# Queries of the expert layer by lists of 128 columns, with 31 single-row slots between them

## The chip, the cores and the metric

The kernel runs on one core of a Trainium2 chip. The metric is the device time of one execution in microseconds; lower is better. Times come from the kernel's timed executions and from one profiled execution.

## What is computed

Two transformer-like blocks run one after the other on 256 tokens of width 2048. The change lies at the end of the second block, in its last projection and its layer of 16,384 experts:

```
x_lat = x_lat + m_lat[2] * (y_l @ w_out[l])
hf = modulate(rmsnorm_2(x_lat, norm_ffn[l]), m_lat[3], m_lat[4])   # h * (1 + scale) + shift
x_lat = x_lat + m_lat[5] * peer_ffn(hf, ...)
# peer_ffn:
q = (ht @ wq).reshape(n, 8, 2, 128)          # 8 heads, 2 halves: 16 lists of 128 columns
s = einsum('nhpc,pkc->nhpk', q, keys)        # 128 scores for each token and list
# top 16 of each half, top 16 of their 256 sums: 16 experts a head, 128 slots a token
gate = softmax(sc)
a = einsum('nd,nhkd->nhk', xb, take(u_tab, eb))
out = einsum('nhk,nhkd->nd', gate * gelu(a), take(v_tab, eb))
```

Each token picks 128 experts (slots). A slot needs its row of U (2048 floats, for a dot product with the token) and its row of V (2048 floats, added to the output with the slot's weight). Then comes a last RMS norm.

## The kernel before

Tokens are handled as two blocks of 128, one token per partition. Dense products stream their weights from memory in chunks of 1 MB (128 partitions x 2048 floats, four chunks to a tile of 512 columns) through four slots. For each chunk ScalarE writes a rounded high part (`hi`, L1273), VectorE the low part (`lo`, L1879), and TensorE does `products` (L691, L692, L695): for each of 4 slices of 128 input rows and each of 2 token blocks three products (high x high, high x low, low x high) with the activations stationary and 512 weight columns moving. SyncE reloads a slot once TensorE has counted the chunk in `split_used`.

At the end of the second block four output tiles (`add_gated` adds them to X and squares them) are followed by the norm, `scaled` (X times the reciprocal root), `queries_turned` (transposes on TensorE), `queries_part` (scale, shift, split in high and low), and 16 chunks of the query product in four tiles. After each tile the 512 query columns are copied to `q_tok`, turned, copied to `q_t`, and multiplied with the keys (L1234); ScalarE copies the scores to `key_s`. `modulated` (L2728, L2730) makes the token rows for the dots. `choose` (top 16 by MAX8, FIND_INDEX8 and MATCH_REPLACE8, then the pick by one-hot products) writes the expert numbers of one or two heads to `idx`. `weights` and `exps` make the softmax. `low_part` (L654) has GpSimd make the low part of four of the 16 chunks.

`GATHERS` is the order in which GpSimd issues the row gathers (indirect DMA, L665). The first 12 slots of token block 0 are gathered as a U row each (1 MB for 128 tokens), into three homes in turn; their V rows come later as single rows. All slots after that are pairs: U and V row together, 2 MB, in seven homes. Four of these homes are the weight slots, two the activations' high and low parts, so they come free only as the last query chunks are done. The last six slots of block 1 are single again. A gather waits until its home has been used (`half_used`): a U row by its dot (`dot`, L2737, on VectorE), a V row or a pair by its sum. The sum of a slot is four TensorE products of 512 columns with a diagonal matrix of the slot's weight (L1259); ScalarE makes that matrix (`diagonal`: gelu L1841, weight L1826, matrix L1829). Before, all sums come after the whole query product. A slot goes: gather, dot, diagonal, sum, next gather into its home.

Of the kernel before, what the change touches and what calls it, by code (L numbers as in the profile page):

```python
# [15 lines left out]
P = 128  # L16
# [58 lines left out]
EARLY_DOTS = (0, 0, 0, 0, 0, 0, 1, 2, 1, 2, 1, 2, 1, 2, 0, 0)  # L75
EARLY_V_AT = 20
DIAGS = 4
POOL_LO = (9, 11, 13, 15)
POOL_LO_AT = (3, 6, 9, 12)
NFIN_AT = 24  # L80
# [66 lines left out]
NCH = S_WQ + OUT_TILES * CPT  # L147
# [66 lines left out]
def homes():  # L214

    places, halves = [], 0
    for kind, b, s in GATHERS:
        if kind == "u" and b == 0:
            places.append(EARLY_HOMES[s % len(EARLY_HOMES)])
# [26 lines left out]
def build(nc, a, out):  # L246
    with ExitStack() as ctx:
# [26 lines left out]
        for name, n in (("ident", P), ("cols", 512), ("modt", 12 * KT), ("small", 512), ("X", NB * D), ("UH", KT * T),  # L274
                        ("UL", KT * T), ("RW", 2 * SLOTS_W * D), ("P", 12288),
                        ("TMP", 6176), ("C", 3584), ("MISC", 1120)):
            region[name] = words
            words += n
# [7 lines left out]
        cols = view("cols", "cols", 0, [512])  # L286
        modt = view("modt", "modt", 0, [6 * KT, 2])
        X = view("X", "X", 0, [NB, D])
        UH = view("UH", "UH", 0, [KT, T], F32R)
        UL = view("UL", "UL", 0, [KT, T], F32R)  # L290
# [120 lines left out]
        assert -(-NCOL // 8) * 8 + P <= 512  # L411
# [5 lines left out]
        q_tok = view("q_tok", "P", 8192, [NB, CW])  # L417
        q_t = view("q_t", "P", 8192 + NB * CW, [2 * GH, T])
        rest = view("rest", "P", 10240, [CK, T])
        key_s = [view("key_s0", "C", 0, [2 * PH, NKEY]), view("key_s1", "TMP", 0, [2 * PH, NKEY])]  # L420
        cand = view("cand", "C", 2048, [GH, TOPK, TOPK])
        hot = view("hot", "C", 2048 + GH * TOPK * TOPK, [GH, TOPK, TOPK])
# [5 lines left out]
        pick_i = view("pick_i", "MISC", 256, [GSTEP], U32)  # L428
        pick_f = view("pick_f", "MISC", 288, [GSTEP])
        exp_f = [view(f"exp_f{i}", "MISC", 320 + 32 * i, [GSTEP]) for i in range(2)]  # L430
# [9 lines left out]
        nfin_rows = view("nfin_rows", "MISC", 400, [CW])  # L440
        sq_out = view("sq_out", "C", 0, [D])
        low_ps, y_ps = [psum[:, 4 * j:4 * j + 4, :].rearrange("p a c -> p (a c)") for j in range(2)]
        rows_g = view("rows_g", "UH", 0, [max(PAIR_AT) + 1, D])
        assert region["UH"] + 14 * D == region["P"] + 4096
# [21 lines left out]
        def half_used(g, half):  # L466

            earlier = [k for k in range(g) if HOMES[k][0] == HOMES[g][0] and (GATHERS[k][0] == "p" or HOMES[k][1] == half)]
            if earlier:
                return dotted(earlier[-1]) if GATHERS[earlier[-1]][0] == "u" else summed(earlier[-1])  # L470
            if HOMES[g] in EARLY_HOMES:
                return sem("xn2_ready"), NB
            return split_used, NCH - SLOTS_W + PAIR_CHUNK[HOMES[g][0]]
# [77 lines left out]
        def hdim(x):  # L551
            return x[:, :].unsqueeze(2)

# [36 lines left out]
        def _(pool):  # L590
# [60 lines left out]
            def low_part(c):  # L651
                s = (S_WQ + c) % SLOTS_W
                pool.wait_ge(hi_ready, S_WQ + c + 1)
                pool.tensor_tensor(WL[:, s, :], raw[:, s, :], WH[:, s, :].bitcast(F32), ALU.subtract).then_inc(sem("pool_lo"), 1)  # L654

            for g, (kind, b, s) in enumerate(GATHERS):
                if g in POOL_LO_AT:
                    low_part(POOL_LO[POOL_LO_AT.index(g)])
# [17 lines left out]
        def _(pe):  # L676
            def products(n, banks, k0, nk, i, per, ah, al, blocks=NB, first=True, last=True, each=None):

                if i is None and n - S_WQ in POOL_LO:
                    pe.wait_ge(sem("pool_lo"), POOL_LO.index(n - S_WQ) + 1)  # L680
                elif i is not None or n:
                    pe.wait_ge(lo_ready, lin(n + 1 - sum(S_WQ + c < n for c in POOL_LO), i, per))
# [514 lines left out]
            linear_among(S_OUT2, Q_OUT2, 0, OUT_TILES, last_turned(), ready=lambda m: (sem("y2_ready"), CK * (m + 1)))  # L1197

            SIDE = ACC[(Q_WQ + 1) % 2]

            def queries_turned(r):
                pe.wait_ge(sem("xn_ready"), NB * xn_made[5] + r + 1)
                if r == 0:
                    for k in range(CK):
                        for b in range(NB):
                            mm = pe.transpose(DB[k][:, b * P:(b + 1) * P], XN2[:, b, k * P:(k + 1) * P], ident[:, :])
                        if k % 2:
                            mm.then_inc(sem("xn_turned"), 1)
                    return
                if r >= 2:  # L1210
                    pe.wait_ge(sem("u_ready"), KT * 4 + CK * (r - 1))
                turn_part(r, XN2, SIDE if r == 1 else DB[2 * (r % 2):2 * (r % 2) + 2])

            def stay_warm(n):
                for _ in range(n):
                    pe.matmul(DB[3][:, 0:NB * P], ident_b[:, :], mask_b[:, :, :].rearrange("p d t -> p (d t)"), start=True, stop=True)

            def queries():
                until = clock(0)
                for r in range(2, CPT):  # L1220
                    queries_turned(r)
                    yield from until(r - 1)
                for t in range(OUT_TILES):
                    yield from until(CPT * (t + 1))
                    pe.wait_ge(acc_free_act, Q_WQ + t + 3)
                    pe.wait_ge(acc_free_dve, Q_WQ + t + 3)
                    turn(lambda j, m: q_tok[:, m % 2, (2 * j + m // 2) * P:(2 * j + m // 2 + 1) * P], DB[0:2], "pq_turned")
                    yield from until(CPT * (t + 1) + 1)
                    pe.wait_ge(sem("q_t_ready"), 2 * (t + 1))
                    if t:  # L1230
                        pe.wait_ge(sem("key_s_ready"), 2 * t)
                    for b in range(NB):
                        for hp in range(2 * GH):
                            mm = pe.matmul(DB[2 + b][:, hp * NKEY:(hp + 1) * NKEY], q_t[:, hp, span(b)],  # L1234
                                           keys[:, hp % 2, :], start=True, stop=True)
                        mm.then_inc(sem("key_ps"), 1)

            stay_warm(40)
            queries_turned(0)
            queries_turned(1)  # L1240
            linear_among(S_WQ, Q_WQ, 0, OUT_TILES, queries(), ready=u_parts(4, 1),
                         each=lambda k: (sem("u_ready"), KT * 4 + k + 1))

            for n, g in enumerate(SUMS):
                kind, b, s = GATHERS[g]
                if n == NFIN_AT:
                    pe.wait_ge(sem("nfin_landed"), 16)
                    pe.wait_ge(sem("key_s_ready"), 2 * OUT_TILES)
# [12 lines left out]
                mm.then_inc(sem("v_done"), 1)  # L1261


        @block.scalar
        def _(act):
# [487 lines left out]
            def outputs():  # L1753
# [5 lines left out]
                for t in range(OUT_TILES):  # L1759
                    if t == OUT_TILES - 1:  # L1760
                        act.activation(spare[:, :], l_ms[0][:, 0:1], ACT.Sqrt)
                    yield from until(CPT * (t + 1) + 2)
                    w = slice(t * CW, (t + 1) * CW)
                    act.wait_ge(acc_free_dve, Q_OUT2 + t + 3)
                    act.activation(XN2[:, 1, w], X[:, 1, w], ACT.Square, accum_out=ss_part[:, 1, t:t + 1]).then_inc(
                        sem("ss_ready"), 1)

            linear_among(S_OUT2, Q_OUT2, 0, OUT_TILES, nothing, outputs())
# [3 lines left out]
            SIDE = ACC[(Q_WQ + 1) % 2]  # L1772

            def queries_part(r):
                if r == 0:
                    act.wait_ge(split_used, S_WQ)
                    for k in range(CK):
                        act.wait_ge(sem("xn_turned"), 8 * 4 + k // 2 + 1)
                        act.activation(UH[:, k, :], DB[k][:, 0:T], ACT.Identity, scale=sc_ffn[:, k:k + 1],
                                       bias=modt[:, 3 * KT + k, 0:1]).then_inc(sem("uh_ready"), 1)  # L1780
                    return
                turned_part(r, 4, SIDE if r == 1 else DB[2 * (r % 2):2 * (r % 2) + 2], lambda k: sc_ffn[:, k:k + 1],
                            lambda k: modt[:, 3 * KT + k, 0:1], S_WQ)

            queries_part(0)
            queries_part(1)
# [1163 lines left out]
```

## Time and profile before

| | before |
|---|---|
| median of the timed runs | 2998.67 us (2998.47 to 3000.13) |
| profiled execution, its own time | 3002.66 us |
| span of its records | 3001.0 us |
| TensorE busy | 2664.9 us, 89% |
| VectorE busy | 2058.4 us, 69% |
| moved by the DMA engines | 958.74 MB |

Times in the rows are microseconds from the span's start. "x16" is a count of records; a float32 product that isn't rounded leaves two records of TensorE, each with its weight load. "[2.03 <-X]" is idle time before a row and what ended it.

### The profile page before, as it was taken

To read this page: it belongs to the slowest core of one execution; us is meant where nothing else is said; L and a number is where in the kernel's file an instruction comes from. 1 tells how busy PE (TensorE), PEld (TensorE's weight loads), DVE (VectorE), ACT (ScalarE), POOL (GpSimd) and SP (SyncE) were. 2 spreads that over 40 slices of the span, in tenths; PEclk is the share of its full clock that TensorE was granted. 3 is DMA by queue.
4 is the path that set the end of the run, shared out by engine and by line. 5 is a ranking of instruction groups with operands and counts; after the bars stand their busy time and mean duration, and the time that the engine had idled before them with its cause. 6 is when DMAs were issued, how large, how long until landed. Compare 5 with 4: busy or idle time off the path is not lost.

```text
span 3001.0 us, 28457 instructions
## 1 busy us (share of the span) xinstructions
PE 2664.9 (89%) x10052; PEld 1807.8 (60%) x10052; DVE 2058.4 (69%) x2510; ACT 1055.7 (35%) x1584; POOL 386.1 (13%) x401
## 2 busy tenths in 40 slices
PE   9999999999999999999999889877777777777773
PEld 7888888888888878888788754322222222222221
DVE  6675689999999987666566894676664554444446
ACT  5544443433333455635454422222222121111111
POOL 0000000000000000000000353211211121111112
PEclk9999999999999999999999999999999999999997
DMA  6454779888888964444354699999999999999997
GB/s 250 170 207 169 282 266 333 330 324 340 333 337 336 343 259 169 150 151 168 130 198 176 229 389 426 428 428 427 429 428 428 428 428 427 428 428 428 427 428 324
DMA packets 99086, 958.74 MB, mean 319 GB/s; under 512 B 11044, under 2 KB 11364, under 8 KB 13608
## 3 DMA queue, kind: packets, MB, share of 16 engines
q0 software_dynamic: 55552, 650.96, 52.2%
q1 hardware_dynamic: 43280, 305.91, 27.6%
q8 instruction: 61, 1.00, 0.1%
q10 hardware_dynamic: 152, 0.53, 0.0%
q14 instruction: 41, 0.34, 0.0%
HBM read 955.23 MB, written 2.13 MB: 319 GB/s over the span
## 4 chain that ended last, share of the span: by engine, by line
PE 59%; DMA 30%; DVE 7%; issue 2%; ACT 2%; POOL 0%; POOLq 0%; SPq 0%; DVEq 0%; ACTq 0%
DMA rows_g<-in_uv_tab_dram,idx 30%; PE bank L691 16%; PE bank L695 16%; PE bank L692 16%; PE bank L1259 6%; DVE rows_g L2737 4%; PE bank L725 1%; PE bank L1074 0%; PE bank L1019 0%; PE bank L733 0%; ACT diag L1829 0%; DMA ctx_x<-in_ctx_dram 0%; DVE split L1879 0%; POOL rows_g L665 0%; DMA raw<-in_wstream_dram 0%
## 5 line engine op out<-in xcount | busy, mean ns | idle before, releaser
L1259 PE MATMUL bank<-rows_g,diag 128*128 128x512 f32 x2000 | 918.7, 605 | 270.9 <-ACT diag L1829 270.9
L2737 DVE CUSTOM_DVE_ANT_0 rows_g<-rows_g,XN 128x2048 f32<-128x2048 f32 x256 | 596.7, 2333 | 542.1 <-DMA rows_g<-in_uv_tab_dram,idx 540.3
L1259 PEld LDWEIGHTS bank<-rows_g,diag 128*128 128x128 f32 x2000 | 365.0, 191 | 824.2 <-issue 824.0
L1879 DVE TENSOR_TENSOR split<-raw,split 128x2048 fp32r<-128x2048 f32 x282 | 645.3, 2289 | 283.6 <-ACT split L1273 277.7
L1273 ACT ACTIVATE split<-raw 128x2048 fp32r<-128x2048 f32 x286 | 547.8, 1917 | 674.3 <-DMA raw<-in_wstream_dram 661.9
L691 PE MATMUL bank<-split,UH 128*128 128x512 f32 x1936 | 764.5, 395 | 3.1 <-DVE split L1879 2.7
L695 PE MATMUL bank<-split,UL 128*128 128x512 f32 x1936 | 755.2, 390 | 0.0
L692 PE MATMUL bank<-split,UH 128*128 128x512 f32 x1936 | 754.6, 390 | 0.0
L665 POOL DMA_INDIRECT rows_g<-in_uv_tab_dram,idx x274 | 301.4, 1100 | 1080.9 <-PE bank L1259 858.5
L691 PEld LDWEIGHTS bank<-split,UH 128*128 128x128 f32 x1936 | 364.4, 188 | 79.1 <-issue 3.2
L695 PEld LDWEIGHTS bank<-split,UL 128*128 128x128 f32 x1936 | 364.1, 188 | 76.5
L692 PEld LDWEIGHTS bank<-split,UH 128*128 128x128 f32 x1936 | 364.3, 188 | 73.9
L1841 ACT ACTIVATE gelu_v<-dots 128x1 f32<-128x1 f32 x238 | 48.2, 203 | 927.7 <-DVE dots L2737 927.6
L2156 DVE CUSTOM_DVE_ANT_0 ada_out<-ada_w,c_row 128x2048 f32<-128x2048 f32 x128 | 292.2, 2283 | 0.0
L606 POOL DMA_DIRECT2D ada_w<-in_ada_dram x96 | 50.7, 528 | 695.0 <-DVE ada_sum L2156 695.0
L691 PE MATMUL bank<-split,FH 128*128 128x512 f32 x320 | 124.6, 389 | 0.2 <-DVE X L2224 0.2
L695 PE MATMUL bank<-split,FL 128*128 128x512 f32 x320 | 124.5, 389 | 0.0
L692 PE MATMUL bank<-split,FH 128*128 128x512 f32 x320 | 124.5, 389 | 0.0
L1829 ACT ACTIVATE diag<-ident,slot_w 128x128 f32<-128x128 f32 x250 | 100.3, 401 | 8.2
L1826 ACT ACTIVATE slot_w<-gelu_v,gate_w 128x1 f32<-128x1 f32 x250 | 73.4, 294 | 7.8
L691 PEld LDWEIGHTS bank<-split,FH 128*128 128x128 f32 x320 | 60.1, 188 | 13.0 <-DVE X L2224 0.4
L695 PEld LDWEIGHTS bank<-split,FL 128*128 128x128 f32 x320 | 60.1, 188 | 12.5
(417 smaller groups left out, 1442.2 us busy)
## 6 DMA issues: line engine op xcount, KB each, us to landing
raw<-in_wstream_dram SPq DMA_DIRECT2D x287, 1024.0 KB, 4.9
ada_w<-in_ada_dram POOLq DMA_DIRECT2D x96, 1024.0 KB, 7.1
rows_g<-in_uv_tab_dram,idx POOLq DMA_INDIRECT x274, 26.2
X<-in_x_dram SPq DMA_DIRECT2D x4, 512.0 KB, 9.4
c_row<-in_c_rows_dram POOLq DMA_DIRECT2D x1, 2048.0 KB, 8.5
ctx_x<-in_ctx_dram POOLq DMA_DIRECT2D x1, 2048.0 KB, 11.6
gb<-mod_rows POOLq DMA_DIRECT2D x2, 1024.0 KB, 5.9
raw<-in_wstream_dram SPq DMA_DIRECT2D x2, 512.0 KB, 6.7
```

Source lines behind the costliest of these rows:

```text
L606: pool.dma_start(ada_w[s][:, :], a["ada"][c]).then_inc(ada_landed[s], 16)
L665: pool.indirect_dma_start(out=whole(g) if kind == "p" else row(g), out_offset=None, in_=a["uv_tab"], in_offset=bass.IndirectOffsetOnAxis(a ...
L691: pe.matmul(o, ah[:, k0 + k, t], wh[:, w], start=first and k == 0, stop=False)
L692: mm = pe.matmul(o, ah[:, k0 + k, t], wl[:, w], start=False, stop=al is None and last and k == nk - 1)
L695: mm = pe.matmul(o, al[:, k0 + k, t], wh[:, w], start=False, stop=last and k == nk - 1)
L1259: mm = pe.matmul(bank[4 * b + c], diag[:, n % DIAGS, :], v[:, c * CW:(c + 1) * CW], start=n in (0, SUMS_0), stop=n + 1 in (SUMS_0, len(SUMS)))
L1273: act.activation(WH[:, n % SLOTS_W, :], raw[:, n % SLOTS_W, :], ACT.Copy).then_inc(hi_ready, 1)
L1826: seq(act.activation(slot_w[:, b, s:s + 1], gelu_v[:, b, s:s + 1], ACT.Copy, scale=gate_w[:, b, s:s + 1]))
L1829: act.activation(diag[:, n % DIAGS, :], ident[:, :], ACT.Copy, scale=slot_w[:, b, s:s + 1]).then_inc(sem("diag_ready"), 1)
L1879: dve.tensor_tensor(WL[:, n % SLOTS_W, :], raw[:, n % SLOTS_W, :], WH[:, n % SLOTS_W, :].bitcast(F32), ALU.subtract).then_inc(lo_ready, 1)
L2156: dve.tensor_tensor_reduce(ada_out[:, :], ada_w[ada_slot(c)][:, :], c_row[:, r, :], 1.0, 0.0, ALU.mult, ALU.add, ada_sum[:, p:p + 1]).then ...
L2737: dve.tensor_tensor_reduce(row(g), row(g), x, 1.0, 0.0, ALU.mult, ALU.add, dots[:, b, s:s + 1]).then_inc(sem("dot_done"), 1)
```

## The change

The weights of the query product become the stationary operand and the turned activations the moving one: 16 lists of 128 query columns, one chunk of 1 MB each, 16 slices x 3 products with 258 columns moving (two blocks of 128 tokens and two columns that hold the shift). The result is already turned, so `q_tok`, its transposes and the four tiles go. X times `sc_row` is turned without the norm, while the last output tile runs; the norm comes back as a row `rms_row` in `query` and as a scale in `scores_kept`. The dummy products (`stay_warm`) and GpSimd's `low_part` go. `choose` does its two one-hot picks together. 31 first slots are single U and V rows, with two homes for U and two for V. The first is summed ahead of list 6, and 30 after the thirds of lists 6 to 15. The first pair, slot 31, is issued behind the V row of slot 30, which waits for the sum of slot 28.

```diff
-PAIR_AT = (4, 6, 14, 8, 10, 0, 2, 17)
+PAIR_AT = (4, 6, 14, 8, 10, 0, 2, 16)
-EARLY, LATE = 12, 6
-EARLY_HOMES = ((2, 0), (2, 1), (PAIRS, 0))
+LATE = 6
+LISTS = 2 * PH
+MIX_AT, MIX = 6, 3
+EARLY = 1 + MIX * (LISTS - MIX_AT)
+U_HOMES, V_HOMES = ((2, 0), (PAIRS, 0)), ((PAIRS, 1), (2, 1))
-NFIN_AT = 24
+NFIN_AT = 64
 def gathers():
-    order = [("u", 0, s) for s in range(EARLY)]
-    for s in range(EARLY, SLOTS):
-        order.append(("p", 0, s))
-        k = s - EARLY_V_AT
-        if k % 2 == 0 and 0 <= k < EARLY:
-            order += [("v", 0, k), ("v", 0, k + 1)]
+    order = [("u", 0, 0)]
+    for s in range(EARLY):
+        if s + 1 < EARLY:
+            order.append(("u", 0, s + 1))
+        order.append(("v", 0, s))
+    order += [("p", 0, s) for s in range(EARLY, SLOTS)]
...
+            def list_part(c, k0, k1):
+                s = (S_WQ + c) % SLOTS_W
+                o = q_bank(c)[:, 0:T + SHIFT]
+                for k in range(k0, k1):
+                    w = slice(k * P, (k + 1) * P)
+                    pe.matmul(o, WH[:, s, w], UHS[:, k, :], start=k == 0, stop=False)
+                    pe.matmul(o, WL[:, s, w], UHS[:, k, :], start=False, stop=False)
+                    mm = pe.matmul(o, WH[:, s, w], ULS[:, k, :], start=False, stop=k == KT - 1)
+                if k1 == KT:
+                    mm.then_inc(split_used, 1)
+            def list_scores(c):
+                pe.wait_ge(sem("q_t_ready"), c + 1)
...
+            last_output_tile()
+            first_list()
+            for c in range(1, MIX_AT):
+                list_begins(c)
+                at = KT // 4 if c == 2 else KT // 2
+                list_part(c, 0, at)
+                if c < 3:
+                    list_scores(c - 1)
+                elif c > 3:
+                    list_scores(c - 2)
+                list_part(c, at, KT)
+            sum_row(0)
+            for c in range(MIX_AT, LISTS):
+                list_begins(c)
+                for j in range(MIX):
+                    list_part(c, KT * j // MIX, KT * (j + 1) // MIX)
+                    if j == 0:
+                        list_scores(c - 2)
+                    sum_row(1 + MIX * (c - MIX_AT) + j)
...
+            lo(S_WQ + 2)
+            query(0)
+            lo(S_WQ + 3)
+            modulated(0)
+            query(1)
+            lo(S_WQ + 4)
+            for _ in choose(0, 0, 0, 1):
+                pass
+            query(2)
+            lo(S_WQ + 5)
+            query(3)
+            modulated(1)
+            weights(0, 0, TOPK)
+            lo(S_WQ + 6)
+            query(4)
+            dve.wait_ge(sem("xn2_ready"), NB)
+            dot(DOTS[0], XN2[:, 0, :])
+            dot(DOTS[1], XN2[:, 0, :])
+            lo(S_WQ + 7)
+            query(5)
+            early = early_choices()
+            for c in range(MIX_AT, LISTS):
+                for j in range(MIX):
+                    n = 2 + MIX * (c - MIX_AT) + j
+                    if n < EARLY:
+                        dot(DOTS[n], XN2[:, 0, :])
+                    next(early, None)
+                    if j == 1:
+                        lo(S_WQ + c + LEAD)
+                query(c)
```

## Rows read from the trace of the kernel before

**Rows 1.** The page: busy shares, then DMA rate in 40 slices.

```profile
PE 2664.9 (89%) x10052; PEld 1807.8 (60%) x10052; DVE 2058.4 (69%) x2510; ACT 1055.7 (35%) x1584; POOL 386.1 (13%) x401
GB/s 250 170 207 169 282 266 333 330 324 340 333 337 336 343 259 169 150 151 168 130 198 176 229 389 426 428 428 427 429 428 428 428 428 427 428 428 428 427 428 324
```

**Rows 2.** Windows: length, busy time of each engine, PE clock, DMA share, GB/s.

```profile
1690.00:1747.30 57.30, 43.90 (x205) 36.23 (x204) 43.66 (x34) 16.03 (x15) 44.58 (x17) 0.91 0.86 325
1747.30:1760.00 12.70, 11.56 (x54) 9.33 (x53) 12.32 (x35) 2.09 (x4) 7.54 (x4) 1.00 0.77 308
1760.00:2975.00 1215.00, 928.05 (x2032) 371.42 (x2032) 681.41 (x974) 250.57 (x773) 268.85 (x258) 0.99 1.01 428
```

**Rows 3.** Timeline of VectorE: two dots of the pair stage.

```profile
2048.96 2.29 DVE L2737 CUSTOM_DVE_ANT_0 rows_g<-rows_g,XN 128x2048 f32<-128x2048 f32 x1 [2.59 <-DMA rows_g<-in_uv_tab_dram,idx]
2053.85 2.29 DVE L2737 CUSTOM_DVE_ANT_0 rows_g<-rows_g,XN 128x2048 f32<-128x2048 f32 x1 [2.59 <-DMA rows_g<-in_uv_tab_dram,idx]
```

**Rows 4.** Timeline of GpSimd: the first gather, a split, the first pair.

```profile
1693.83 2.08 POOL L665 DMA_INDIRECT rows_g<-in_uv_tab_dram,idx  x1 [130.93 <-DVE idx L2722]
...
1727.68 4.61 POOL L654 TENSOR_TENSOR split<-raw,split 128x2048 fp32r<-128x2048 f32 x1
...
1747.27 2.82 POOL L665 DMA_INDIRECT rows_g<-in_uv_tab_dram,idx  x1 [0.16 <-issue]
```

**Rows 5.** Timeline of TensorE and VectorE around the norm and the first choice.

```profile
1637.60 4.54 PE L1216 MATMUL bank<-mask_b,ident_b 128*128 128x256 bf16 x40
1682.88 0.49 DVE L2680 MAX8 top_v<-key_s 128x8 f32<-128x128 f32 x2 [0.16 <-DVE XN L2730]
1692.66 0.17 DVE L2722 CAST idx<-pick_f 128x16 uint32<-128x16 f32 x1
```

**Rows 6.** Groups by line: count, busy, mean ns, idle before.

```profile
L2737 DVE CUSTOM_DVE_ANT_0 rows_g<-rows_g,XN 128x2048 f32<-128x2048 f32 x256 | 596.7, 2333 | 542.1 <-DMA rows_g<-in_uv_tab_dram,idx 540.3
L1879 DVE TENSOR_TENSOR split<-raw,split 128x2048 fp32r<-128x2048 f32 x282 | 645.3, 2289 | 283.6 <-ACT split L1273 277.7
L1273 ACT ACTIVATE split<-raw 128x2048 fp32r<-128x2048 f32 x286 | 547.8, 1917 | 674.3 <-DMA raw<-in_wstream_dram 661.9
raw<-in_wstream_dram SPq DMA_DIRECT2D x287, 1024.0 KB, 4.9
```

**Rows 7.** Timeline of TensorE and its weight loads: spacing of products.

```profile
1565.97 0.39 PE L695 MATMUL bank<-split,UL 128*128 128x512 f32 x1
1566.19 0.39 PE L691 MATMUL bank<-split,UH 128*128 128x512 f32 x1
...
1133.33 0.28 PE L966 MATMUL bank<-UL,wg_s 128*32 128x256 f32 x1
1133.44 0.28 PE L966 MATMUL bank<-UH,wg_s 128*32 128x256 f32 x1
...
1719.98 1.95 PE L1234 MATMUL bank<-keys,q_t 128*128 128x128 f32 x16
```

**Rows 8.** All weight loads of that line: ns least, median, most.

```profile
L1234 PEld LDWEIGHTS bank<-keys,q_t x64: 188/192/333, 1680.8 to 1770.1; 128*128 128x128 f32 x64
```

**Rows 9.** Chain that ended last: start, length, what.

```profile
1693.83 7.93 DMA rows_g<-in_uv_tab_dram,idx
...
1720.43 8.56 DMA rows_g<-in_uv_tab_dram,idx
...
1735.28 9.46 DMA rows_g<-in_uv_tab_dram,idx
...
1796.76 20.85 PE bank L1259 x48
```

**Rows 10.** Chain near the end: a sum, then the next gather.

```profile
2955.42 3.69 PE bank L1259 x8
...
2959.90 2.56 POOL rows_g L665
```

**Rows 11.** Windows with transfers of 8 KB a partition alone.

```profile
1000.00:1040.00 40.00, 40.00 (x182) 33.24 (x181) 37.25 (x34) 14.47 (x8) 3.69 (x7) 1.00 0.96 368
1704.00:1708.00 4.00, 0.00 (x0) 0.00 (x0) 3.48 (x4) 0.00 (x0) 1.92 (x1) 0.70 1.01 428
```

More of the change, by code:

```diff
@@ L677, in products @@
             def products(n, banks, k0, nk, i, per, ah, al, blocks=NB, first=True, last=True, each=None):
[L679 to L682, printed above, removed]
+                if i is not None or n:
+                    pe.wait_ge(lo_ready, lin(n + 1, i, per))
                 wh, wl = WH[:, n % SLOTS_W, :], WL[:, n % SLOTS_W, :]
@@ L1195, in last_turned @@
                 yield
[L1197 to L1209, printed above, removed]
+            linear_among(S_OUT2, Q_OUT2, 0, OUT_TILES - 1, last_turned(), ready=lambda m: (sem("y2_ready"), CK * (m + 1)))
@@ L1210, in queries_turned, with scaled_turned @@
+            def scaled_turned(r):
+                pe.wait_ge(sem("xs_ready"), r + 1)
                 if r >= 2:
                     pe.wait_ge(sem("u_ready"), KT * 4 + CK * (r - 1))
[L1212 to L1244, printed above, removed]
+                turn_part(r, XN2, DB[2 * (r % 2):2 * (r % 2) + 2])
+            def last_output_tile():
+                n, q = S_OUT2 + CPT * (OUT_TILES - 1), Q_OUT2 + OUT_TILES - 1
+                pe.wait_ge(acc_free_act, q + 1)
+                pe.wait_ge(acc_free_dve, q + 1)
+                for m in range(CPT - 1):
+                    products(n + m, LAST_ACC, m * CK, CK, None, 0, UH, UL, first=m == 0, last=False)
+                    scaled_turned(m)
+                m = CPT - 1
+                pe.wait_ge(lo_ready, n + m + 1)
+                wh, wl = WH[:, (n + m) % SLOTS_W, :], WL[:, (n + m) % SLOTS_W, :]
+                for b in range(NB):
+                    t = slice(b * P, (b + 1) * P)
+                    for k in range(CK):
+                        w = slice(k * CW, (k + 1) * CW)
+                        pe.matmul(LAST_ACC[b], UH[:, m * CK + k, t], wh[:, w], start=False, stop=False)
+                        pe.matmul(LAST_ACC[b], UH[:, m * CK + k, t], wl[:, w], start=False, stop=False)
+                        mm = pe.matmul(LAST_ACC[b], UL[:, m * CK + k, t], wh[:, w], start=False, stop=k == CK - 1)
+                    mm.then_inc(sem("last_out_ps") if b == 0 else split_used, 1)
@@ L1822, in _, with exps @@
[L1822 to L1825 removed]
+            scaled_high(CPT - 1)
+            act.wait_ge(sem("rms_spread"), 1)
+            act.activation(rms_row[:, :], DB[0][:, 0:T], ACT.Copy).then_inc(sem("rms_kept"), 1)
+            def exps(b, first, n):
+                mine = slice(first, first + n)
+                act.wait_ge(sem("idx_ready"), chosen(b, first))
+                act.activation(gate_w[:, b, mine], gate_w[:, b, mine], ACT.Exp).then_inc(sem("exp_done"), 1)
@@ new lines, in scores_kept, with diagonal @@
+            def scores_kept(c):
+                act.wait_ge(sem("key_ps"), c + 1)
+                for b in range(NB):
+                    act.activation(key_s[b][:, c, :], score_bank(c)[:, b * NKEY:(b + 1) * NKEY], ACT.Copy,
+                                   scale=rinv[:, b:b + 1]).then_inc(sem("key_s_ready"), 1)
+            def diagonal(n):
+                g = SUMS[n]
+                kind, b, s = GATHERS[g]
+                act.wait_ge(*dotted(g if kind == "p" else GATHERS.index(("u", b, s))))
+                seq(act.activation(gelu_v[:, b, s:s + 1], dots[:, b, s:s + 1], ACT.Gelu_apprx_tanh))
+                act.wait_ge(sem("gates_ready"), chosen(b, s))
@@ new lines, in _, with last_gated @@
+            linear_among(S_OUT2, Q_OUT2, 0, OUT_TILES - 1, add_gated, outputs())
+            for m in range(CPT):
+                lo(S_OUT2 + CPT * (OUT_TILES - 1) + LEAD + m)
+                if m:
+                    scaled_low(m - 1)
+            def last_gated(b):
+                w = slice((OUT_TILES - 1) * CW, D)
+                x = X[:, b, w]
+                link(dve.tensor_tensor(g_tmp[:, b, :], LAST_ACC[b][:, :], gb1[:, w], ALU.mult))
+                ins = dve.scalar_tensor_tensor(x, x, x_rms[:, b:b + 1], g_tmp[:, b, :], ALU.mult, ALU.add)
+                if b == 0:
+                    link(ins)
+                    square(OUT_TILES - 1)
+                    scaled(b, OUT_TILES - 1)
+                    return
+                ins.then_inc(acc_free_dve, 1)
+                dve.wait_ge(acc_free_dve, Q_OUT2 + OUT_TILES + 2)
+                scaled(b, OUT_TILES - 1).then_inc(sem("xs_ready"), 1)
@@ L2749, in later_choices @@
             def later_choices():
-                for k in range(1, NB * GROUPS):
+                for k in range(2, NB * GROUPS):
                     yield from choose(k // GROUPS, k % GROUPS)
-                    yield from pause(GROUP_STEPS - 7)
-                    weights(k // GROUPS, k % GROUPS)
+                    yield from pause(GROUP_STEPS - 6)
+                    weights(k // GROUPS, GSTEP * (k % GROUPS), GSTEP)
                     yield
-            later, rows = later_choices(), modulated()
@@ L2757, in _ @@
-            for m in range(OUT_TILES * CPT):
-                if m + LEAD not in POOL_LO:
-                    lo(S_WQ + m + LEAD)
-                if m < 2:
-                    queries_part(m + 2)
-                elif m < 6:
-                    next(rows)
-                if m == 5 or m == 14:
-                    for _ in choose(0, 0, 0 if m == 5 else 1, 1):
-                        pass
-                for g in range(sum(EARLY_DOTS[:m]), sum(EARLY_DOTS[:m + 1])):
-                    dot(g, XN2[:, 0, :])
-                if m % CPT == CPT - 1:
-                    dve.wait_ge(split_used, S_WQ + m + 1)
-                    to_q((Q_WQ + m // CPT) % 2, m // CPT)
+            lo(S_WQ + 2)
@@ new lines, in _ @@
+            query(5)
+            early = early_choices()
+            for c in range(MIX_AT, LISTS):
+                for j in range(MIX):
+                    n = 2 + MIX * (c - MIX_AT) + j
+                    if n < EARLY:
+                        dot(DOTS[n], XN2[:, 0, :])
[3 more added lines that the diff above has]
+                query(c)
+            for _ in early:
+                pass
+            later = later_choices()
@@ L2902, in layout @@
     put(S_OUT2, chunks(np.concatenate([mixed[D_SGU + D_ML:], mixed[:D_SGU + D_ML]])))
-    put(S_WQ, chunks(first["peer_wq_2"]))
+    put(S_WQ, first["peer_wq_2"].reshape(KT, P, LISTS, P).transpose(2, 1, 0, 3))
     def down_cols(x):
```

351 lines of the change are left out of this document (196 added, 155 removed).

## The prediction

> **What bounds the kernel now.** I read the page first [rows 1]: TensorE is busy 89% of the span, but from slice 24 on the DMA rate stands at 428 GB/s to the end. The windows [rows 2] put an edge on it: 428 GB/s with a DMA share of 1.01 from 1760 to 2975 us, while TensorE is busy 928 of 1215 us. So there are two regimes. Up to about 1760 us TensorE bounds; after it the row gathers do, at one pair (128 x 16 KB = 2.097 MB, 4.90 us at 428 GB/s) per slot. Two dots in a row start 4.89 us apart [rows 3]. What a faster query stage is worth is therefore read from one event: when the first pair is issued, and how many slots are left then. Before it is 1747.3 us [rows 4], with 12 single V rows and 244 slots left, which is 250 slots' worth of bytes.
>
> **The price of the end.** After the change the first pair is issued behind V row 30, that is when sum 28 is done; call it T. Then 225 slots and one V row are left, 225.5 slots' worth, 24.5 fewer. That is 24.5 x 4.89 = 119.8 us. Before, the DMA queues had run low at that moment (308 GB/s in the 12.7 us behind it [rows 2], 3.6 us lost); after, pairs queue directly behind single rows, of which about one more is under way then (half of 2.45 us to all of it). Net 2 us gained. The homes behind it come free in time: V row 30 and the first two pairs are 12 us of transfers, and the last list ends about 8 us after T. The stage from there on and the tail are unchanged. So end = 3001 + (T - 1747.3) - 119.8 - 2 = T + 1131.9, and T breaks even at 1869.1.
>
> **The head, up to the first gather.** Before, 40 dummy products start at 1637.6 when the output tiles are done [rows 5]. After, three transposed parts run inside the last tile (about 1 us each) and it ends at 1640.7. List 0 needs the last part turned, split and the norm's row: two half lists, then a chain of small operations like that of before; I put its end at 1648.8. One list is 48 products of 258 columns. Their spacing is not in the trace in that shape. At 512 columns it is 0.227 us, at 256 columns with 32 weight columns 0.114, and 16 passes with full 128-column loads and about the same streaming time take 1.95 us with the last one's latency, 0.112 each [rows 7]. Each of those loads has a duration of 188 ns and more [rows 8], so loads of that length do overlap at a spacing of 0.112. I take 0.115, 5.5 us a list; the bounds are 0.112 and, if the loads ran one behind the other, 0.19, 9.1 us a list.
>
> The first choice needs lists 0 and 1, and their scores (ahead of the last three quarters of list 2): 1648.8 + 5.5 + 0.5 + 1.4 + 0.5, and 0.9 for ScalarE's copies: 1657.6. VectorE has low parts at 2.29 us each [rows 6], the modulation of block 0 and two queries before it and arrives at 1657.8. The choice took 9.9 us [rows 5]; five of its ten pick operations go, at most 1.2 us. It ends at 1666.5, and the first gather starts 1.0 us later as now: 1667.5 instead of 1693.8 [rows 4]. TensorE needs 5 x 5.5 us and scores to 1678.3. VectorE (choice, two low parts, three queries, modulation, weights) reaches dot 0 at 1675.5 and dot 1 at 1678; a gelu with its table load and the diagonal follow. Sum 0 runs from about 1680.4 to 1683.9. V row 1 goes out at 1680.3, behind U row 2, which waits for dot 0, and sum 1 ends at 1691.8. The weights are no brake: a chunk lands in 4.9 us, hi 1.9, lo 2.3 [rows 6], 9.1 us against three lists of slack. The extra scaling by VectorE in the output tiles (1.3 us a tile) lies under TensorE.
>
> **The mix, 27 further sums to T.** Call the period of one slot p: T = 1691.8 + 27 p, so break-even is p = 6.57. Four things bound p from below. TensorE: 16 products (1.84), a sum (48 records in 20.85 us [rows 9], 8 a slot: 3.48), a third of the scores (0.17), switches 0.1: 5.6 us. VectorE: a dot 2.3 [rows 6], a third of a low part and of a query, choices: 4.1. DMA: two rows and a third of a chunk, 2.45 MB. At 428 GB/s, which single rows reach for 4 us, that is 5.72 us. Over 40 us the best stage with 8 KB transfers has 368 GB/s at a share of 0.96 [rows 11]; that would be 6.65. The stage of the early U rows has 325 at 0.86 [rows 2], scaled to a full share 378 and 6.48. I lean to the faster end: that 40 us window is one where TensorE, not DMA, is full.
>
> The fourth is the ring of two V homes. A sum ends, the next gather starts 0.8 us later [rows 10], its row lands a trip L after that, and the sum takes 3.5: 2 p = 0.9 + L + 3.5. L for single rows was 7.9, 8.6 and 9.5 us [rows 9], each the first of three issued at once, with 2.1 to 2.8 us of it GpSimd's own time, lengthened by the splits on GpSimd (4.6 us each [rows 4]) that now go. U rows go out about 2.7 us ahead of their V rows, as a dot is done sooner than a sum, so the two queue little on each other. Weight chunks (2.45 us of transfer every third slot) hold both up. I take L = 8.2, p = 6.3. U's ring is shorter (0.9 + L + 2.3, plus up to 2 us behind other VectorE work), so it follows. T = 1691.8 + 27 x 6.3 = 1861.9, end 2993.8: 7.2 us less than 3001.0. The profiled execution stands 4.0 us above the median of the runs and its span 2.3; I carry the 7.2 to the median: 2991.5.
>
> **What is priced at nothing.** The transposes of queries, their copies and the dummy products are gone with the serial chain they stood in; that is inside the head's and the mix's times. The cheaper picks of the later choices, NFIN_AT and the changed softmax groups lie under the 4.89 us transfers of the pair stage, where VectorE is busy 681 of 1215 us [rows 2]; without that cover the picks would be worth 1.2 us a choice.
>
> **The rivals.** (1) The ring closes faster than I think, L about 7: then DMA and TensorE bound at p = 5.75, T = 1847, end 2979, time 2976.7. For it: the splits on GpSimd go. Against: it needs a sustained 425 GB/s of 8 KB transfers. Chance 0.15.
> (2) No change: L between 8.3 and 9.2 (p 6.35 to 6.79), or the DMA engines saturate at the 378 GB/s above. T about 1867, time 2997. For it: two of the three trips are that long and the load on DMA is higher in the mix. Chance 0.25.
> (3) Slower: the trip exceeds 9.2 us. Its place is V's ring: GpSimd issues in order, VectorE's work stretches its descriptor writing, and a third of all slots share the engines with a chunk. With L = 9.6, p = 7.0, T = 1880.8, time 3010.4. It decides from p = 6.79. For it: the 9.46 us trip, and no stage of 8 KB transfers above 368 GB/s for long. Against: that trip was issued with two more rows behind it and next to a split. Chance 0.21.
> (4) The weight loads aren't hidden under 258 columns: a list takes 9.1 us. The head is 20 us longer up to sum 0, and p = 3.03 + 3.48 + 0.2 = 6.73; T = 1712.7 + 181.7 = 1894.4, end 3026, time 3024. Against it stands the spacing of 0.112 [rows 7, 8]. Chance 0.07.
> The Trainium skill's page "TensorE: Matmul & The Clock Gate" says, in "Part 3: Packing small matmuls", that a weight load overlaps products in flight only when its row group differs; with an estimate from its columns / 1.2 for the load, 107 ns, and 107 for the stream, a list would take 10.3 us and this rival would come out some 20 us longer. By that rule, too, 512 columns would be spaced 0.32 us apart; the trace has 0.227, so it does not agree.
>
> **How the numbers follow.** My forecast (p 5.9 to 6.34) has 0.32, rival 1 0.15, rival 2 0.25, rival 3 0.21, rival 4 0.07. About 0.2% of the time, 6 us, is what a measurement can tell from nothing. Faster by over 0.2%: 0.32 + 0.15 = 0.47. Within: 0.25. Slower: 0.21 + 0.07 = 0.28. The range reaches from rival 1 to a p of 7.2: 2976 to 3016; outside lie rival 4, the worst of rival 3, and a head that is much shorter than counted. The forecast's own range is 2982 to 2993.
>
> **What would show it.** First gather at 1667 (within 4); list products spaced 0.112 to 0.12; sums in the mix 6.3 us apart, TensorE idle about 0.7 us before each and released by the row's DMA, not by the diagonal; DMA near 390 GB/s there; first pair near 1862; the pair stage unchanged at 4.89. Wrong if sums are released by ScalarE's diagonal (then VectorE's order is the brake), if the first choice is late, or if the clock of TensorE falls in the idle gaps of the mix.

## The result, and the profile after

The kernel after takes 3037.76 us (median of 4 runs, 3035.61 to 3038.68), the one before 2998.86 beside it: a ratio of 1.0123, 95% interval 1.0111 to 1.0136. It is slower by 1.2%, 46 us above my forecast and outside my range. The profiled execution took 3038.19 us, its span is 3036.4.

The page of the kernel after, busy shares and DMA rate in 40 slices [rows 1]:

```profile
PE 2701.6 (89%) x10368; PEld 1822.8 (60%) x10368; DVE 2052.8 (68%) x2494; ACT 1050.7 (35%) x1599; POOL 377.7 (12%) x416
GB/s 246 168 193 167 282 262 314 317 331 317 334 333 325 333 293 167 145 147 175 121 170 204 291 358 348 399 428 427 429 428 427 428 428 428 428 428 428 428 428 329
```

TensorE is busy 37 us longer, and 428 GB/s starts later. Windows of the stages [rows 2], with the same columns:

```profile
1712.00:1906.00 194.00, 173.78 (x735) 108.76 (x735) 113.83 (x178) 51.69 (x123) 74.29 (x58) 0.95 0.91 351
1940.00:2975.00 1035.00, 778.64 (x1688) 305.04 (x1688) 569.33 (x752) 209.07 (x650) 205.86 (x211) 1.00 1.01 428
```

The pair stage is what it was, 428 GB/s. The whole loss lies ahead of it, so I followed the events on which my sum stands: the first gather, V row 30 and the first pair, on GpSimd's timeline [rows 4].

```profile
1697.41 2.47 POOL L673 DMA_INDIRECT rows_g<-in_uv_tab_dram,idx  x1 [107.06 <-DVE idx L2820]
...
1904.95 1.03 POOL L673 DMA_INDIRECT rows_g<-in_uv_tab_dram,idx  x1 [6.08 <-PE bank L1299]
1906.28 0.94 POOL L673 DMA_INDIRECT rows_g<-in_uv_tab_dram,idx  x1 [0.30 <-issue]
```

The first gather is 29.9 us later than my 1667.5. The list products do what I expected of them: this is TensorE's timeline inside a list [rows 7].

```profile
1675.11 0.28 PE L1236 MATMUL bank<-UHS,split 128*128 128x258 f32 x1
1675.22 0.28 PE L1237 MATMUL bank<-ULS,split 128*128 128x258 f32 x1
1675.35 0.28 PE L1235 MATMUL bank<-UHS,split 128*128 128x258 f32 x1
1675.46 0.28 PE L1236 MATMUL bank<-UHS,split 128*128 128x258 f32 x1
```

The delay is older than the change. VectorE begins to evacuate the last output tile but one at 1616.04 us before and at 1646.02 after, 30.0 us later, and up to there TensorE has the same products in both programs. What differs is their pace. The timeline of the kernel after where [rows 7] had 0.22 us between two products:

```profile
1565.76 0.40 PE L697 MATMUL bank<-split,UH 128*128 128x512 f32 x1
1566.00 0.40 PE L698 MATMUL bank<-split,UH 128*128 128x512 f32 x1
1566.24 0.39 PE L701 MATMUL bank<-split,UL 128*128 128x512 f32 x1
1566.47 0.39 PE L697 MATMUL bank<-split,UH 128*128 128x512 f32 x1
1566.70 0.40 PE L698 MATMUL bank<-split,UH 128*128 128x512 f32 x1
1566.93 0.40 PE L701 MATMUL bank<-split,UL 128*128 128x512 f32 x1
```

From first to last start it is 1.17 us for five products, 0.234 each; before it is 0.2267. The groups of lines from 600 to 1000 us, where TensorE has no idle time in either trace and a granted clock of 1.00, tell which products:

```profile
L701 PE MATMUL bank<-split,UL 128*128 128x512 f32 x377 | 149.7, 397 | 0.0
L698 PE MATMUL bank<-split,UH 128*128 128x512 f32 x378 | 149.4, 395 | 0.0
L697 PE MATMUL bank<-split,UH 128*128 128x512 f32 x378 | 149.2, 395 | 0.0
L697 PE MATMUL bank<-split,FH 128*128 128x512 f32 x192 | 74.7, 389 | 0.0
```

Before, all of them take 389 to 390 ns, and 389 of each of the first three fit into these 400 us. Products with FH stationary are as before; those with UH and with UL are 5 to 8 ns longer. There are 5400 of them on the page. Their instructions are the same in both programs. What the diff does to them is in the arena's list: `cols` and `MISC` shrink, and UH and UL each get 32 words (128 bytes a partition) of padding ahead. UH now lies 64 bytes lower than before and everything behind it 64 bytes higher, so that the distance from UH to UL and to the weight slots is 128 bytes off, modulo 256. UL and the weight slots keep their distance.

### The profile page after: what moved, and what is told of

Same layout as the page of the kernel before. It is cut to its first block, busy times and chain, and to the rows that moved or that the text cites. A ratio compares the mean times of both kernels' runs of the same rounds, so it can differ in the third digit from the quotient of the medians.

```text
span 3036.4 us, 29124 instructions
## 1 busy us (share of the span) xinstructions
PE 2701.6 (89%) x10368; PEld 1822.8 (60%) x10368; DVE 2052.8 (68%) x2494; ACT 1050.7 (35%) x1599; POOL 377.7 (12%) x416
## 4 chain that ended last, share of the span: by engine, by line
PE 62%; DMA 31%; DVE 3%; issue 2%; ACT 1%; POOL 0%; POOLq 0%; SPq 0%; DVEq 0%
DMA rows_g<-in_uv_tab_dram,idx 31%; PE bank L698 16%; PE bank L701 16%; PE bank L697 16%; PE bank L1299 7%; DVE rows_g L2825 2%; PE bank L731 1%; PE bank L739 1%; PE bank L1080 0%; PE bank L1025 0%; ACT diag L1876 0%; DMA raw<-in_wstream_dram 0%; POOL rows_g L673 0%; PE bank L936 0%; ACT slot_w L1873 0%
## 5 line engine op out<-in xcount | busy, mean ns | idle before, releaser
L1299 PE MATMUL bank<-rows_g,diag 128*128 128x512 f32 x2000 | 931.6, 609 | 293.3 <-ACT diag L1876 269.9
L2825 DVE CUSTOM_DVE_ANT_0 rows_g<-rows_g,XN 128x2048 f32<-128x2048 f32 x256 | 586.8, 2292 | 551.8 <-DMA rows_g<-in_uv_tab_dram,idx 550.9
L1950 DVE TENSOR_TENSOR split<-raw,split 128x2048 fp32r<-128x2048 f32 x286 | 654.5, 2290 | 304.9 <-ACT split L1337 300.9
L697 PE MATMUL bank<-split,UH 128*128 128x512 f32 x1800 | 717.7, 399 | 1.2 <-DVE split L1950 1.2
L701 PE MATMUL bank<-split,UL 128*128 128x512 f32 x1800 | 714.7, 397 | 0.0
L698 PE MATMUL bank<-split,UH 128*128 128x512 f32 x1800 | 712.1, 396 | 0.0
L673 POOL DMA_INDIRECT rows_g<-in_uv_tab_dram,idx x293 | 312.6, 1067 | 1097.4 <-PE bank L1299 909.8
L698 PEld LDWEIGHTS bank<-split,UH 128*128 128x128 f32 x1800 | 338.8, 188 | 82.5
L697 PEld LDWEIGHTS bank<-split,UH 128*128 128x128 f32 x1800 | 338.8, 188 | 80.8 <-issue 2.5
L701 PEld LDWEIGHTS bank<-split,UL 128*128 128x128 f32 x1800 | 338.5, 188 | 79.9
L1235 PE MATMUL bank<-UHS,split 128*128 128x258 f32 x256 | 85.1, 332 | 0.0
L1237 PE MATMUL bank<-ULS,split 128*128 128x258 f32 x256 | 72.4, 283 | 0.0
```

The source lines that it names most:

```text
L673: pool.indirect_dma_start(out=whole(g) if kind == "p" else row(g), out_offset=None, in_=a["uv_tab"], in_offset=bass.IndirectOffsetOnAxis(a ...
L697: pe.matmul(o, ah[:, k0 + k, t], wh[:, w], start=first and k == 0, stop=False)
L698: mm = pe.matmul(o, ah[:, k0 + k, t], wl[:, w], start=False, stop=al is None and last and k == nk - 1)
L701: mm = pe.matmul(o, al[:, k0 + k, t], wh[:, w], start=False, stop=last and k == nk - 1)
L1235: pe.matmul(o, WH[:, s, w], UHS[:, k, :], start=k == 0, stop=False)
L1299: mm = pe.matmul(bank[4 * b + c], diag[:, n % DIAGS, :], v[:, c * CW:(c + 1) * CW], start=n in (0, SUMS_0), stop=n + 1 in (SUMS_0, len(SUMS)))
```

## The experiments

**1. Addresses alone.** Theory A: this move of the buffers is the cause. Rival B: something in the new stage is. The kernel before, with the layout of after and no other edit:

```
-  ("cols", 512) ... ("UH", KT * T), ("UL", KT * T)
+  ("cols", 464) ... ("UH", 32 + KT * T), ("UL", 32 + KT * T)
-  UH = view("UH", "UH", 0, ...)    UL = view("UL", "UL", 0, ...)    rows_g = view("rows_g", "UH", 0, ...)
+  UH = view("UH", "UH", 32, ...)   UL = view("UL", "UL", 32, ...)   rows_g = view("rows_g", "UH", 64, ...)
```

> The kernel before, with nothing changed but where its buffers lie: cols, the padding words in front of UH and UL, and so every address behind them, as in the changed kernel (UH 64 bytes lower, UL, the weight slots and all behind them 64 bytes higher). Theory A (address): products whose stationary operand lies in UH or UL are spaced 0.233 instead of 0.227 us for where these buffers lie; then the first gather comes near 1725, and the time is 3030 to 3036. Rival B (the program: its other instructions, their fetching, or the order in the new output and query code cost the products): addresses alone change nothing, 2999 within 3.

Measured: 3038.4 us, ratio 1.0134 (1.0117 to 1.0151), 2 us above what A said, with the same count and durations per group as after: 378, 395 to 397 ns, FH 389. The first gather starts at 1723.96. The old program at the new addresses takes the time of the new program. A is shown, B is out.

**2. Everything behind `cols` shifted alike,** by 192 bytes (only `cols` 464):

> The kernel before with cols 48 words shorter: every buffer behind it 192 bytes lower, so that all keep their distances and all start at an odd multiple of 64 bytes. Theory A1 (what counts is where the stationary operand starts, in steps of 128 or 256 bytes): spacing 0.233 at UH and UL, 3030 to 3036, and FH and FL unchanged, which would be odd as they lie at an odd multiple of 64 too. Theory A2 (what counts is the distance between the operands' buffers): spacing 0.227, 2999.

Measured: 2999.97 us (one run), products of 389 to 390 ns. Moving all buffers by 192 bytes costs nothing; with run 1, it is how far apart they lie that counts.

**3. The kernel after, with the distances of before.** `small` 400 and a second padding ahead of UL bring UH, UL and the weight slots back to equal addresses modulo 256:

```
-  ("small", 512) ... ("UL", PAD + KT * T)
+  ("small", 400) ... ("UL", 2 * PAD + KT * T)
-  UL = view("UL", "UL", PAD, ...)       ULS = view("ULS", "UL", 0, ...)
+  UL = view("UL", "UL", 2 * PAD, ...)   ULS = view("ULS", "UL", PAD, ...)
```

> The changed kernel with UH and UL put back to the addresses, modulo 256 bytes, of the kernel before (a shorter small region, 32 more words of padding in front of UL). Theory A: spacing 0.227 again, first gather near 1664, the mix unchanged at 6.6 us a slot, first pair near 1872, time 3002 to 3007. Rival B: unchanged, 3037.

Measured: 3004.22 us, ratio 1.0012 (1.0003 to 1.0022), products of 389 to 390 ns. The padding had cost some 33 us. The change proper gains nothing: it is slower by 0.12%, with an interval of 0.03 to 0.22%. GpSimd's first gather starts at 1663.22, the first pair at 1873.50.

**4. Which distance.** Three runs on the kernel before, with `small` 448 and 64 words given back in paddings, so that the weight slots keep their address modulo 256:

```
4a   UL alone + 128 bytes:        ("UL", 64 + KT * T), view at 32
4b   UH and UL both + 128 bytes:  ("UH", 32 + KT * T), view at 32; ("UL", 32 + KT * T), view at 0
4c   UH alone + 64 bytes:         ("UH", 16 + KT * T), view at 16; ("UL", 48 + KT * T), view at 48
```

> The kernel before with UL alone moved by 128 bytes (modulo 256) against UH and the weight slots. Theory A (a load of stationary columns meets the reading of the weight columns under way, where the two buffers lie 128 bytes apart modulo 256; with UH off two loads of three are met, with UL off one): spacing of the products 0.230 us, half of the 34 us, so 3016 us. Theory B (any unequal pair costs the whole): 0.2333 us and 3034 us. Theory C (only UH counts): 0.2267 us and 2999 us.

> The kernel before with UH and UL both moved by 128 bytes (modulo 256), so that they keep their distance to one another and only that to the weight slots changes. Theory A: all three loads are met, 0.2367 us a product and 3050 us. Theory B: 0.2333 us and 3034 us. Rival D (the distance of UH to UL is what costs): 0.2267 us and 2999 us.

> The kernel before with UH alone moved by 64 bytes (modulo 256) against UL and the weight slots. If 128 bytes is what costs: 0.2267 us a product and 2999 us. If any distance but zero costs: 0.2333 us and 3034 us. If it grows with the distance: 0.230 us and 3016 us.

Measured: UL alone 3022.79 us, ratio 1.0072 (1.0055 to 1.0089); both 3031.98, 1.0098 (1.0082 to 1.0115); UH by 64 bytes 3034.08, 1.0108 (1.0091 to 1.0125). Theory A's detail fell (it said 3016, 3050). With UL alone, B fell, which wanted the whole for any unequal pair, and C, which wanted nothing. D fell too: UH and UL side by side, off the weights alone, cost nearly the whole. The groups of the run with UL alone off say what does hold:

```profile
L695 PE MATMUL bank<-split,UL 128*128 128x512 f32 x382 | 151.7, 397 | 0.0
L692 PE MATMUL bank<-split,UH 128*128 128x512 f32 x381 | 151.0, 396 | 0.0
L691 PE MATMUL bank<-split,UH 128*128 128x512 f32 x382 | 149.4, 391 | 0.0
```

The order is L691, L692, L695 for each k and token block, and the next product's load starts with a product: in the trace of before a product L692 starts at 701.397 and the load for L695 at 701.400. L695 has UL as its own stationary columns; under L692, UL is being loaded; under L691, UH is. So theory X: a product is slow if the buffer it has in the array, or the one loaded while it streams, is off the weight columns it reads. With UL off that is two of three, 22 of 33 us; with UH off, or both, all three. X is made from these runs, so it needs one of its own.

**5. Theory X, put to the test.** UL alone by 64 bytes (view at 16):

> The kernel before with UL alone moved by 64 bytes (modulo 256). Theory X, formed on the three runs before it (a product is slow where its own stationary buffer, or the one whose load falls into it, lies at another offset modulo 256 than the weight columns that it reads; so two of three with UL off, three of three with UH off): the product UH by high parts stays at 390 ns in the trace, the two others at 395 to 397, 2/3 of the 34 us, 3022 us. Rival (the size depends on the distance in bytes: 64 costs another amount than 128 for UL): clearly under 3015 or over 3030 us.

Measured: 3023.03 us, ratio 1.0074 (1.0058 to 1.0090), and in the groups:

```profile
L695 PE MATMUL bank<-split,UL 128*128 128x512 f32 x381 | 151.3, 397 | 0.0
L692 PE MATMUL bank<-split,UH 128*128 128x512 f32 x381 | 149.3, 392 | 0.0
L691 PE MATMUL bank<-split,UH 128*128 128x512 f32 x381 | 148.8, 391 | 0.0
```

The time and the count of 381 are those of 128 bytes, as X says. Its detail did not come: L692 was to take 395 to 397 ns and takes 392. The ends of products are modelled, so I also took the starts, up to 1630 us, as mean ns from each product to the next, gaps over 330 ns left out; the excess is that of the three together over before:

| | L691 | L692 | L695 | excess |
|---|---|---|---|---|
| before | 229.2 | 226.9 | 227.0 | |
| addresses of after (run 1) | 234.8 | 232.8 | 234.5 | 19.0 |
| UL + 128 (4a) | 229.4 | 232.4 | 233.9 | 12.6 |
| UH and UL + 128 (4b) | 234.5 | 232.5 | 232.6 | 16.5 |
| UH + 64 (4c) | 234.2 | 232.4 | 233.7 | 17.2 |
| UL + 64 (5) | 230.6 | 229.3 | 235.3 | 12.1 |

With UL 128 bytes off, X fits each of the three. With UL 64 bytes off the sum is the same, but most of it falls on the product with UL as its own stationary columns (8.3 ns; 2.4 on L692, 1.4 on L691). So the total by buffer is shown, two thirds for UL and nearly the whole for UH, while X as a rule for single products is borne out by UL at 128 bytes only. Nor does X say why the excess runs from 16.5 to 19.0 where all three are slow. What happens in the memory no run shows.

**6. The mix: is it TensorE's clock?** In the kernel after, the chain that ended last has these rows in the mix [rows 9] (start, length, what):

```profile
1713.08 6.54 PE bank L1299 x8
...
1731.41 10.51 DMA rows_g<-in_uv_tab_dram,idx
1741.97 5.41 PE bank L1299 x8
...
1773.98 8.91 DMA rows_g<-in_uv_tab_dram,idx
1782.94 5.40 PE bank L1299 x8
...
1830.91 3.72 PE bank L1299 x8
```

Sum 0 takes 6.54 us and four later ones 5.4 in place of 3.7, each behind a wait for its row, with a granted clock that falls to 0.88 in the mix's first 38.6 us. A product of the mix's sums spans 592 ns in the median and 1193 at the most, about twice as long: those stand at the lower of the two levels (1.2 against 2.4 GHz). The run fills such waits, on top of run 3, with products that add zeros:

```
+ if 0 < n < EARLY:
+     for _ in range(6):
+         pe.matmul(bank[0][:, 0:NB * P], zero[:, 0:1].to_broadcast([P, P]), mask_b[...], start=False, stop=False)
  pe.wait_ge(*row_landed(g))
```

> The kernel after with its buffers laid as before (3004.2 us, single V rows 6.62 us apart in the mix), with six products of 256 bf16 columns by zeros (some 0.65 us together) put ahead of each sum of the mix's single rows but the first. Theory of the clock (after a long wait for a row TensorE is granted half the clock, and four sums take 5.4 us in place of 3.6): the waits shrink, no sum is over 4 us, the period falls to 6.4 us and the first pair comes 6 us earlier, 2998 us. Rival (the period is the row's way and the sum; a filler only delays the sums that don't wait): the period is 6.6 to 7.0 us, 3004 to 3015 us, with or without half-clock sums.

Measured: 3002.83 us, ratio 1.0010 (1.0000 to 1.0019). Windows of the mix, run 3 above, this run below:

```profile
1700.00:1870.00 170.00, 149.29 (x640) 93.97 (x639) 99.54 (x166) 45.50 (x106) 67.95 (x50) 0.96 0.91 349
```

```profile
1700.00:1870.00 170.00, 162.36 (x815) 108.19 (x814) 101.90 (x168) 46.42 (x109) 61.68 (x51) 1.00 0.92 353
```

The clock stays at 1.00 and in the chain no sum but sum 0 (6.20) is over 4 us, as foretold. The first pair comes 4.4 us earlier in the profile (1869.10 against 1873.50), but the period, from sum 1's end (1690.71) to sum 28's (1867.05) over 27, is 6.53 us, not 6.4, and the medians differ by 1.4 us with intervals that overlap. The time lies between the theory's 2998 and the rival's 3004. The half clock is real, and with a filler of 0.65 us a slot against it next to nothing is won: a sum takes 0.27 us less in the mean (3.63 against 3.90), but a row that has landed waits 0.24 us longer for TensorE, and the long trips stay (10.3, 11.1, 9.7, 8.1 us in this run's chain).

**7. Fewer single rows.** My own sum prices a slot at 4.89 us in the pair stage and at p in the mix, so a single row is worth its place only while it lies under the list. With m of them a list takes the longer of 5.75 + 3.45 m (TensorE) and 6.62 m (the ring). Less the 4.89 m that are saved later: m = 3, 19.9 - 14.7 = 5.2 us; m = 2, 13.2 - 9.8 = 3.4 us; 18 us over ten lists. On top of run 3:

```
- MIX_AT, MIX = 6, 3        HEAD1_AT, GROUP1_AT = 3, 15
+ MIX_AT, MIX = 6, 2        HEAD1_AT, GROUP1_AT = 3, 11
```

> As a1_realigned, with two slots between halves of a list instead of three between thirds: 21 single slots instead of 31. If a slot in the mix costs 6.6 us for the ring of its V row (gather, trip, sum) and a pair 4.89 later, ten slots fewer cost 10 x 4.89 behind the mix and save 10 x 6.6 in it, unless TensorE (24 products at 0.12 and a sum, 6.6 us a slot) has become longer: 2984 to 2992. If instead the DMA engines are what the mix waits for (0.93 busy), the mix moves the same bytes at the same rate and the time stays within 4 us of a1_realigned.

Measured: 2992.25 us, ratio 0.9971 (0.9961 to 0.9981), faster than both kernels, at the edge of what was expected, and 12.0 us under run 3 for the 18 of that sum. That the mix only moves bytes at a fixed rate, which wanted a time within 4 us of run 3, is out. Why 6 of the 18 are missing isn't settled. Its profiled execution is the longest of its nine, 3000.29 us: there nine pairs of slots take 13.09 us (the sum had 13.2), but others 13.3 to 14.4, and one row trips for 12.7 us and its sum takes 6.6.

**8. Both,** with fillers ahead of sums 1 to 10 only:

> The version with two single rows a list (2992.3 us) with six products by zeros (0.65 us) ahead of sums 1 to 10. Theory of the clock: no sum over 4 us (one took 6.61 there, 3 us too long), the first pair comes 2 to 3 us earlier, 2989 to 2990 us. Rival: TensorE sets this mix's pace (5.75 + 2 times 3.45 us a list), so the fillers cost 0.65 us each where nothing waits, up to 6 us together: 2993 to 2998 us.

Measured: 2996.31 us, ratio 0.9988 (0.9979 to 0.9997). The window of its mix:

```profile
1684.00:1812.00 128.00, 128.00 (x689) 91.61 (x688) 88.00 (x156) 41.02 (x86) 51.47 (x36) 1.00 0.91 354
```

TensorE is full and at full clock. This profile is a short one (span 2990.8), but the median is 4 us over run 7's, with intervals that just touch. It is the rival's case: in this profile a list with fillers takes 14.44 us, and the later ones without them 13.1 to 13.8, so fillers cost their 0.65 us each where nothing waits. With two rows a list TensorE mostly sets the pace.

## Why the prediction was wrong

**The step that failed** is the one that I took without a sentence: that all ahead of the last output tile stays. The head starts from 1637.6 and 1640.7 as if nothing before it could move. The diff moves UH, UL and the weight slots against each other, and 5400 products there are 5 to 8 ns longer on average. Run 1 shows that this alone gives 3038 us, run 3 that without it the change gives 3004. None of my rivals had it; that the end came out slower is not rival 3 or 4. A second step failed too, the mix's period, forecast 6.3 us and measured 6.62; it is taken apart below.

**The ledger against the forecast's span of 2993.8:**

- Sum 1 ends at 1725.3, forecast 1691.8: 33.5 us late. 30 of it stood at 1646.02 already; most of the rest is sum 0 at the lower clock, 6.54 us for 3.5.
- 27 periods: sum 28 ends at 1904.14, p = 6.62 for 6.3, so 8.7 us more. That is a p of rival 2's band.
- The end: 1904.14 + 1131.9 = 3036.0; the span is 3036.4.

**The price of the end** was right to 0.7 us in five kernels, if T is the end of the sum ahead of the last single V gather (each slot fewer adds 4.89): run 3 1871.3, so 3003.2 (3003.1 measured); run 6 1867.1, 2999.0 (2998.7); run 7 1818.3 with ten slots more, 2999.1 (2998.6); run 8 1810.6, 2991.4 (2990.8). The first pair itself comes 2.1 us after that, which I had put at nothing, so the other terms of that sum (the 2 us that I called gained) must have been short by as much; no run separates them.

**The head** was right once the addresses are: in run 3 the first gather starts at 1663.22 (forecast 1667.5) and sum 1 ends at 1690.3 (1691.8), though sum 0 takes 5.37 us. That is luck in part. VectorE begins on the last output tile but one at 1612.15 in that profile and at 1616.04 in the one of before, and the kernel before with all buffers shifted alike (run 2) has 1612.33, so one profile stands some 4 us from another before the change begins. The step from the last tile to the first gather (26.8 us by my times, 26.6 measured) was right; sum 1 comes 53.7 us behind the tile, for 51.1, most of it sum 0.

**The list products** are spaced 0.12 us, 5.75 us a list, for my 0.115 and 5.5. Rival 4 is refuted, and with it the rule that stood beside it: by that rule of the Trainium skill's page "TensorE: Matmul & The Clock Gate", "Part 3: Packing small matmuls", a list would take 10.3 us, and here too the trace does not agree.

**The mix** is the mis-sized term, but not in the term that I doubted. The cause that I named holds: V's ring, not VectorE and not DMA's rate alone, sets the period; the waits of the kernel after in the mix (us in total, times, longest) are

```profile
POOL rows_g L673 <- PE bank L1299: 96.0, 25, 7.2
ACT gelu_v L1871 <- DVE dots L2825: 73.2, 18, 6.6
DVE rows_g L2825 <- DMA rows_g<-in_uv_tab_dram,idx: 69.5, 24, 6.2
...
PE bank L1299 <- DMA rows_g<-in_uv_tab_dram,idx: 23.3, 15, 4.2
```

GpSimd waits for the sums, the sums for rows: in 18 of the 27 slots a sum starts within 0.12 us of its row's landing. The ring's parts, mean us over V rows 2 to 28 of each profile:

| | sum n-2 to gather | trip L | landed to sum n | sum n | 2 p |
|---|---|---|---|---|---|
| forecast | 0.9 | 8.2 | 0 | 3.5 | 12.6 |
| after | 0.91 | 7.98 | 0.39 | 3.91 | 13.2 |
| run 3 | 0.90 | 8.18 | 0.44 | 3.90 | 13.4 |
| run 6 (fillers) | 0.90 | 7.85 | 0.68 | 3.63 | 13.1 |

So the trip that I took was not too short: 7.98 us in the mean, between 5.5 and 10.9. Rival 2's number came without its reason, an L of 8.3 to 9.2. Two other terms were too small. The sum takes 3.6 to 3.7 us from first start to last end where I had 3.5, the spacing of the products alone, and four take 5.4, a danger that I named at the end and priced at nothing. And a row that lands while TensorE is at list products waits, over 0.5 us in 9 of 27 slots, which I put at nothing. The chain shows trips of 7.3 to 10.5 us, but it has only those that were waited for. The rows of U take longer, 9.0 us in the median, and did not set the pace. The mix moved 351 GB/s, not the 390 I foretold; over 38.6 us it never had more than 381.

So with the addresses mended the change is 2.7 us over the kernel before (3004.2, and 3001.5 measured beside it) where I forecast 7.2 under. The 9.9 us between are the 27 periods, 6.70 each in that profile, 10.9 us, less 1.5 of the head. That is rival 2's case by its number, which had 0.25. (The low end of my forecast's own range is misreckoned: a p of 5.9 gives 2980.7, not 2982.)

## What to carry to other kernels

Read a diff's list of buffers as an edit of its own: before costing the new stage, work out how the old stages' operands move against each other, and for products with f32r operands keep stationary and moving buffers at equal addresses modulo 256 bytes, the only case that was free of cost here; a padding of 32 words ahead of UH and of UL cost 33 us, more than everything the change was about. An untouched stage whose groups have other durations, or another count in a window that is full in both traces, is the sign to look for, and the old program at the new addresses is the run that settles it. When work is moved ahead of a bandwidth-bound stage, price each piece at what it takes there less what it saves later: here two rows a list were better than three by 12 us. And split a period that you forecast into its parts before you blame one: here the part in doubt was right, and two that were taken as known were not.

## What the runs showed of the hardware that was not expected

A product of 512 f32r columns with 128 stationary columns is spaced 0.227 us when UH, UL and the weight slots lie at equal addresses modulo 256 bytes. With the addresses of after it is 5.6 to 7.5 ns more, 2.8% (378 products in 400 us for 389). With UL 64 or 128 bytes off the three products of a step take 12.1 and 12.6 ns more together, with UH off (64 bytes, or 128 together with UL) 16.5 to 17.2; other distances were not tried. The page "SBUF — State Buffer" of the Trainium skill, section "A bandwidth-pool intuition that's wrong (but worth ruling out)", gives TensorE a second, independent read port for its weight loads. These runs do not agree with full independence, as the pace depends on how the buffers of the two reads lie to each other; that the ports are the place of it is not shown. Section "SBUF: two separate sides" says that TensorE's port waits on no other engine; no run here bears on that.

The list products, where the roles are exchanged (weights stationary, UHS and ULS streaming 258 columns), have the same 0.12 us at both layouts, in the kernel after and in run 3. Their slices are 1032 bytes apart, so the distance to the weights moves on by 8 bytes with each k, and neither layout holds them at one distance.
